# A hybrid decoder step: row projection and recurrence levels in one block, columns projected first

## The reference

```
def even_project(x, pos, lb, w_in):
    h = x @ w_in
    hq, hf, hi, hg, nq, ncmp, nslc, nwin, ngate = jnp.split(h, np.cumsum(EVEN_SPLITS)[:-1], axis=-1)
    f = lb + (1.0 - lb) * jax.nn.sigmoid(hf.astype(jnp.float32))
    hg_q = jax.nn.silu(hq.astype(jnp.float32)).reshape(B, T, HG_HEADS, HG_DK)
    hg_k = 1.0 - f
    hg_lf = jnp.log(f)
    hg_v = hi.astype(jnp.float32).reshape(B, T, HG_HEADS, HG_DV)
    ...
def hgrn2_chunk(S0, q, k, v, lf):
    b = jnp.cumsum(lf, axis=1)
    diff = b[:, :, None] - b[:, None, :]
    decay = jnp.exp(jnp.where(causal[None, :, :, None, None], diff, -jnp.inf))
    a = jnp.einsum('bthk,btshk,bshk->bhts', q, decay, k)
    o = jnp.einsum('bhts,bshv->bthv', a, v) + jnp.einsum('bthk,bhkv->bthv', q * jnp.exp(b), S0)
    S = jnp.exp(b_end)[..., None] * S0 + jnp.einsum('bshk,bshv->bhkv', k * jnp.exp(b_end[:, None] - b), v)
```

## Time and profile before

| | us |
|---|---|
| median of 3 runs | 2469.85 (2465.31 to 2473.75) |
| profiled execution | 2469.82 |
| its span (first to last instruction) | 2468.0 |
| TensorE busy | 1848.0 (75%) |
| VectorE busy | 1529.8 (62%) |
| ScalarE busy | 553.8 (22%) |
| GpSimd busy | 721.3 (29%) |
| DMA, mean | 304 GB/s |

### The profile page before, as it was taken

How to read it: one execution, slowest core, us unless ns; L and a number is a source line. 1 busy time by engine, 2 the same in 40 slices (tenths; PEclk the granted TensorE clock), 3 DMA queues, 4 the chain that set the end, 5 groups by cost and what they waited for, 6 DMA issues and landing times.

```text
span 2468.0 us, 18705 instructions
## 1 busy us (share of the span) xinstructions
PE 1848.0 (75%) x5407; PEld 851.8 (35%) x5407; DVE 1529.8 (62%) x3388; ACT 553.8 (22%) x1694; POOL 721.3 (29%) x612
## 2 busy tenths in 40 slices
PE   8968289899668786686876787685668678688765
PEld 3456155534313222343422342232333233223221
DVE  0053733138498947666578679748757965647976
ACT  0010222101223311222114222313312322212222
POOL 4000000000234533233323334423323434344442
PEclk9985556598789997778988899897889989899988
DMA  8300120300588999999999999999899999999997
GB/s 282 97 18 1 38 69 0 135 35 1 211 334 344 421 420 392 356 370 375 415 403 373 405 415 420 404 413 359 312 369 412 420 373 419 411 421 421 416 382 304
DMA packets 144944, 750.82 MB, mean 304 GB/s; under 512 B 22077, under 2 KB 46537, under 8 KB 63817
## 3 DMA queue, kind: packets, MB, share of 16 engines
q0 software_dynamic: 84480, 608.21, 61.0%
q1 hardware_dynamic: 60360, 141.41, 15.6%
HBM read 743.96 MB, written 5.60 MB: 304 GB/s over the span
## 4 chain that ended last, share of the span: by engine, by line
DMA 22%; DVE 20%; PE 18%; issue 5%; SPq 1%; ACT 1%; POOL 1%; PEldq 1%; DVEq 1%; PEld 0%; ACTq 0%
DMA uv<-in_experts_dram,slots 14%; PE ps L1933 9%; DVE uv L1841 7%; PE ps L525 4%; DVE acc L1855 2%; DMA last_w<-in_odd_w_in_dram 2%; DMA first_w<-in_odd_w_in_dram 2%; PE ps L846 1%; PE ps L685 1%; SPq L1546 1%; PE ps L874 1%; DVE route_s L1675 1%; DMA out_dil_p_dram<-dil_val 1%; DMA last_w<-in_peer_w_q_dram 1%; DMA sample_rows<-in_peer_sub_keys_dram 1%
## 5 line engine op out<-in xcount | busy, mean ns | idle before, releaser
L1823 POOL DMA_INDIRECT uv<-in_experts_dram,slots x576 | 690.7, 1199 | 1685.2 <-PE ps L1933 923.2
L1933 PE MATMUL ps<-uv,diag 128*128 128x512 f32 (+1 forms) x1664 | 897.1, 681 | 286.5 <-ACT diag L1909 222.1
L1841 DVE CUSTOM_DVE_ANT_0 uv<-uv,x 128x1024 f32<-128x1024 f32 x512 | 621.4, 1224 | 360.2 <-DMA uv<-in_experts_dram,slots 278.6
L1933 PEld LDWEIGHTS ps<-uv,diag 128*128 128x128 f32 (+1 forms) x1664 | 314.2, 202 | 783.4 <-issue 446.7
L1887 ACT ACTIVATE gelu<-dot 128x2 f32<-128x2 f32 x288 | 58.6, 203 | 1042.4 <-DVE dot L1841 1041.9
L1855 DVE SCALAR_TENSOR_TENSOR acc<-uv,wgt,acc 128x1024 f32<-128x1024 f32 x155 | 198.4, 1280 | 2.0 <-ACT wgt L1896 2.0
L1896 ACT ACTIVATE wgt<-gate,gelu 128x1 f32<-128x1 f32 x576 | 138.1, 287 | 57.0 <-SPq L2036 23.9
L1909 ACT ACTIVATE diag<-const,wgt 128x128 f32<-128x128 f32 (+1 forms) x416 | 148.7, 386 | 9.4
L1841 DVE CUSTOM_DVE_ANT_0 uv<-uv,xs 128x1024 f32<-128x1024 f32 x64 | 78.1, 1226 | 42.2 <-DMA uv<-in_experts_dram,slots 38.3
L441 PE MATMUL ps<-even_w,xT 128*128 128x512 f32 (+3 forms) x240 | 98.4, 566 | 0.6 <-PEq L288 0.6
L525 PE MATMUL ps<-last_w,xT 128*128 128x512 f32 x160 | 77.3, 626 | 19.1 <-DMA last_w<-in_odd_w_in_dram 16.4
(11 more groups left out here) (430 smaller groups left out, 1931.8 us busy)
## 6 DMA issues: line engine op xcount, KB each, us to landing
sample_cache<-in_cache_dil_kv_dram SPq DMA_DIRECT2D x64, 256.0 KB, 7.5
sample_w_in<-in_odd_w_in_dram SPq DMA_DIRECT2D x12, 1024.0 KB, 11.6
first_w<-in_odd_w_in_dram SPq DMA_DIRECT2D x12, 1024.0 KB, 11.4
last_w<-in_odd_w_in_dram SPq DMA_DIRECT2D x12, 1024.0 KB, 13.4
uv<-in_experts_dram,slots POOLq DMA_INDIRECT x576, 10.7
even_w<-in_even_w_in_dram SPq DMA_DIRECT2D x8, 1024.0 KB, 8.5
uv<-in_peer_w_q_dram SPq DMA_DIRECT2D x8, 1024.0 KB, 13.9
first_w<-in_peer_w_q_dram SPq DMA_DIRECT2D x8, 1024.0 KB, 10.0
```

The source lines that it names most:

```text
L1823: self.k.nc.gpsimd.indirect_dma_start(out=self.uv[:, s % RING, :], out_offset=None, in_=self.table, in_offset=bass.IndirectOffsetOnAxis(ap ...
L1841: ins = nc.vector.tensor_tensor_reduce(self.uv[:, s % RING, 0:D], self.uv[:, s % RING, 0:D], x, 1.0, 0.0, ALU.mult, ALU.add, self.dot[:, g ...
L1933: last = nc.tensor.matmul(k.bank(c)[0:m, :], self.diag[:, s % RING, 0:m], self.uv[:, s % RING, D + 512 * c:D + 512 * (c + 1)], start=(j == ...
```

## The change

The columns are projected before the rows, in a block with the caches' stage and without the rows. The rows move into the recurrence, whose two blocks become one: TensorE does ten pieces of the rows, then one level product after every two pieces, then the rest. Rows use banks 0, 1 and 7 and ScalarE alone for their copies; levels use banks 2 to 5, so the sample tile shares two banks with tile 0 and waits for VectorE's use of them. The rows' buffer `even_w` has three slots and lies at a fixed address, and `q_b` lies in the sigmoid's buffer. The early loads of caches, columns and rows are issued in `load_inputs`, in front of its wait.

```
-def load_inputs(k, x_prompt, x_sample, const):
+def load_inputs(k, x_prompt, x_sample, const, following):
...
             sp.dma_start(k.x[0:NS, 2, :], x_sample.rearrange("b t d -> (b t) d")).then_inc(loaded, 16)
+            for stage in following:
+                stage.parts.pop("early loads")(sp)
             sp.wait_ge(loaded, 48)
...
-def project_rows(k, name, w, widths, out, wbuf, tiles=(0, 1, 2), banks=ALL_BANKS):
+def project_rows(k, name, w, widths, out, wbuf, tiles=(0, 1, 2), banks=ALL_BANKS, by=("vector", "scalar")):
...
-                            pe.wait_ge((v_out, s_out)[(i - nb) % 2], (i - nb) // 2 + 1)
+                            pe.wait_ge(outs[(i - nb) % n_by][0], (i - nb) // n_by + 1)
...
-        q_b = k.sbuf("hg_q_b", [128, C4, DEC_B, NS], ctx=ctx)
+        q_b = sg[:, :, :].rearrange("p a t -> p (a t)")[:, 0:C4 * DEC_B * NS].rearrange("p (c b t) -> p c b t", c=C4, b=DEC_B)
...
+        def level_bank(t, odd):
+            return k.bank(4 + odd if t == 1 else 2 + odd)
+
+        def levels(pe):
+            for n in range(len(LEVELS) + 1):
+                for t in lanes(n):
+                    pe.wait_ge(factors[t] if n else s["prepared"], n or 1)
+                    if t == 2:
+                        pe.wait_ge(factors[0], n + 1)
+                    elif t == 0 and 0 < n <= s_levels:
+                        pe.wait_ge(factors[2], n)
+                    for hd in range(HG):
...
+                    last.then_inc(products[t], 1)
+                    yield
...
         with nc.Block() as block:
+            @block.sync
+            def _(sp):
+                rows.parts["sync"](sp)
+
             @block.tensor
             def _(pe):
                 pe.wait_ge(inputs.landed, 16 * inputs.loads)
-                nc.tensor.transpose(k.bank(0)[:, 0:12], inputs.gamma[:, :], k.c("ident")[0:12, 0:12]).then_inc(s["gamma_turned"], 1)
+                nc.tensor.transpose(k.bank(6)[:, 0:12], inputs.gamma[:, :], k.c("ident")[0:12, 0:12]).then_inc(s["gamma_turned"], 1)
+                dense, small_work = rows.run("tensor", pe), levels(pe)
+                for _ in range(10):
+                    next(dense)
+                for _ in small_work:
+                    for _ in range(2):
+                        next(dense)
+                for _ in dense:
+                    pass
...
                 nc.scalar.activation(small[:, 16:28], small[:, 16:28], ACT.Exp).then_inc(s["bounds_exp"], 1)
+                for _ in rows.run("scalar", act):
+                    pass
...
+                nc.vector.memset(k.pad[:, :], 0.0).then_inc(s["prepared"], 1)
...
+            wbuf = k.nc.alloc_sbuf_tensor_at("even_w", [128, 3, 4, 512], F32, offset=TOP - 4 * 3 * 4 * 512)
+            out = lambda j, t: h[0:ROWS[t], t, 512 * j:512 * j + widths[j]]
+            rows = project_rows(k, "even", w_in[:, 1024:], widths, out, wbuf, (0, 1, 2), (0, 1, 7), ("scalar",))
             with ExitStack() as load:
-                wbuf = k.sbuf("even_w", [128, 4, 4, 512], ctx=load)
                 wbuf_T = k.sbuf("even_wT", [128, 3, 8, 256], ctx=load)
-                out = lambda j, t: h[0:ROWS[t], t, 512 * j:512 * j + widths[j]]
-                rows = project_rows(k, "even", w_in[:, 1024:], widths, out, wbuf)
                 columns = project_cols(k, "even_T", w_in, 1024, hT, wbuf_T)
-                alone(k, transpose_x(k, "x0"), following=(rows,))
-                alone(k, caches.stage(k, state_inputs, a), rows, following=(columns,))
-                alone(k, columns)
-            recurrence(k, h, hT, cat, state_inputs, fin, new, a["hg_norm_g"][0], o["state_prompt"], o["state_sample"])
+                prepare = caches.stage(k, state_inputs, a)
+                load_inputs(k, a["x_prompt"], a["x_sample"], a["const"], (prepare, columns, rows))
+                alone(k, transpose_x(k, "x0"))
+                alone(k, prepare, columns, loads=(columns, prepare))
+            recurrence(k, h, hT, cat, state_inputs, rows, fin, new, a["hg_norm_g"][0], o["state_prompt"], o["state_sample"])
```

More of the change, by code:

```diff
@@ L399, in project_rows @@
     landed = [k.sem(name, f"w_landed{i}") for i in range(slots)]
-    half_done, product, v_out, s_out = [k.sem(name, n) for n in ("half_done", "product", "v_out", "s_out")]
-    n_t = len(tiles)
+    half_done, v_out, s_out = [k.sem(name, n) for n in ("half_done", "v_out", "s_out")]
+    n_t, n_by = len(tiles), len(by)
+    copies = {"vector": (v_out, nc.vector.tensor_copy), "scalar": (s_out, nc.scalar.copy)}
+    outs = [copies[engine] for engine in by]
     loads = [(j, half) for j in range(len(widths)) for half in range(2)]
@@ L450, in take_out @@
             for what, *rest in tick:
-                if what == "leave" and rest[0] % 2 == side:
+                if what == "leave" and rest[0] % n_by == side:
                     i = rest[0]
@@ L457, in take_out @@
             yield
-    stage.on("vector")(lambda dve: take_out(dve, 0, v_out, nc.vector.tensor_copy))
-    stage.on("scalar")(lambda act: take_out(act, 1, s_out, nc.scalar.copy))
+    for side, engine in enumerate(by):
+        stage.on(engine)(lambda eng, side=side: take_out(eng, side, *outs[side]))
     return stage
@@ L1002, in load, with recurrence @@
             sp.dma_start(self.state[:, c, :, :], state[0, :, 2 * c:2 * c + 2].rearrange("b h k v -> (h k) b v")).then_inc(self.landed, 16)
-def recurrence(k, h, hT, cat, inputs, fin, new, norm_g, state_prompt, state_sample):
+def recurrence(k, h, hT, cat, inputs, rows, fin, new, norm_g, state_prompt, state_sample):
     nc, step = k.nc, k.dve_steps
@@ L1014, in recurrence @@
         "gamma_turned", "bounds_diff", "bounds_exp", "sigmoid", "cross_product", "spread", "state_product", "out_product",
-        "state_ready", "squares", "root", "gates")}
+        "state_ready", "squares", "root", "gates", "prepared")}
     products, factors = [[k.sem(f"hg_{n}_tile{t}") for t in range(TILES)] for n in ("products", "factors")]
@@ L1044, in _ @@
                 dve.wait_ge(s["gamma_turned"], 1)
-                step(nc.vector.tensor_copy(small[:, 0:12], k.bank(0)[:, 0:12]))
+                step(nc.vector.tensor_copy(small[:, 0:12], k.bank(6)[:, 0:12]))
                 step(nc.vector.tensor_tensor(small[:, 12:16], small[:, 0:4], small[:, 4:8], ALU.max))
@@ L1105, in _ @@
                         if t < 2:
-                            src = k.ps[:, 2 * t:2 * t + 2, :].rearrange("p a (b t) -> p (a b) t", t=128)
+                            src = k.ps[:, 2 + 2 * t:4 + 2 * t, :].rearrange("p a (b t) -> p (a b) t", t=128)
                             nc.vector.copy_predicated(att[:, t, :, :], bc(masks[:, n, :], 1, HG), src)
@@ L1126, in _ @@
                 dve.wait_ge(s["cross_product"], 1)
-                step(nc.vector.tensor_copy(cross[:, :, :], k.ps[:, 6:8, :].rearrange("p a (b t) -> p (a b) t", t=128)))
+                step(nc.vector.tensor_copy(cross[:, :, :], k.ps[:, 2:4, :].rearrange("p a (b t) -> p (a b) t", t=128)))
                 tN = tot[len(LEVELS) % 2]
@@ L2192, in build @@
         k.level_masks = a["level_masks"]
-        load_inputs(k, a["x_prompt"], a["x_sample"], a["const"])
         w_out = a["even_w_out"][0]
```

40 lines of the change are left out of this document (15 added, 25 removed).

## The result

The changed kernel takes 2436.88 us (median of 4 runs, 2433.36 to 2443.95), the kernel before 2468.51 us beside it: a ratio of 0.9873, 95% interval 0.9845 to 0.9902, 31.6 us less. The forecast was 2452.2 us with a range of 2439 to 2463. The sign was right; the gain is nearly twice the forecast, and the time lies 2 us under the range.

A forecast was written before the change was run, and what follows sets the result against it. TensorE bounds the projections, VectorE and ScalarE the gates, VectorE the levels. Replacing 187.5 us by 5.0 + 41.5 + 124.6 = 171.1, with 1.2 more off, saves 17.6 from 2469.82: 2452.2 us, range 2439 to 2463.

The forecast's parts named there:

- Behind it: Key transposes and first head, right after dense work: 1.2 us taken off, bounds 0 and 15.
- rival C: Recurrence heads keep the full clock after the dense block: 15 us less instead of 1.2, 2438 us; chance 0.04.
- The start: Seven more load issues before SyncE's wait, held by the queue, delay turning x by 5.0 us, bounds 0 and 7.4.
- Rival B: At the start, SyncE isn't held, or the queue holds more: 5.0 us less, 2447.2 us; chance 0.08.
- the sentence of the Trainium skill cited beside the term: Many descriptors can be emitted before their generating cost shows; by that the start's issues are short, sum 5.0 us lower.
- The columns' block: Column projection with GpSimd's page gathers, which end the block: 41.5 us, not 32.0; TensorE idles 9.5 us.
- The merged block: Row projection interleaved with gates and level products: 124.6 us, of it 98.43 rows, 24 products, 0.9 slow clock.
- D: Merged block: small products in the dense stream lower the clock, so slower; 2493 us if a third fell; chance 0.04.
- E: Merged block: no overlap, TensorE waits each round or weight loads come late; 2468 us; chance 0.04.

The follow-up runs named there:

- late: Changed kernel with GpSimd's 32 page gathers moved from the columns' block into the merged block; 2437.98 us, ratio 0.9862 to the kernel before.
- behind: Changed kernel with only the loads of x ahead of SyncE's wait, pages and first column and row weights issued later; 2433.78 us, ratio 0.9839.
- gap: Changed kernel with eight VectorE fills between key transposes and heads, TensorE idle there; 2464.51 us, ratio 0.9966 to the kernel before.
- bridge: Kernel before, plus ten dense products with unused results behind the cross product, ahead of key transposes and heads; 2461.04 us, ratio 0.9971.
- att_fill: Changed kernel plus sixteen dense unused products under VectorE's rotation of queries and keys, ahead of the attention; 2443.90 us, ratio 0.9888.

## Why the prediction was right in sign and wrong in size

**The step that failed** is the term "Behind it", 1.2 us with bounds 0 and 15: it left seven of the eight heads at half clock. The 1.2 is what the key transposes got (3.83 us with their barrier before, 2.54 after, 1.3 less). The heads got another 12.6 us (31.94 before, 19.32 after) and what lies behind them 1.3. The mechanism was on the list as rival C, with 0.04, and against it stood one reading: at 222 to 230 the heads run at 0.50 with TensorE wholly busy. That stretch lies behind the fall. The row shows that heads at 0.50 stay there; it doesn't show that they can't have the full clock, which the first head of the same kernel has (207.70 to 210.10). The question was whether the heads keep the level when they follow dense work, and on that the kernel before has no row, since nothing dense stands ahead of its heads. So C couldn't be refuted from it, and with the bound of 15 us written down it belonged inside the range. Experiments 1 and 2 show the cause from both sides: the old kernel with dense work right ahead has fast heads, the new one with a gap of 11 us has slow ones. But dense work followed by two short idle times, which is what the changed kernel has, doesn't always keep the level: `late` has the same and loses it. With `late`'s heads the term would have been 1.4 us (70.7 from keys to cat, against 72.2 before), as forecast. That the changed kernel keeps the level in each of its profiles is shown; why it does and `late` doesn't is open, and nothing in the change was made for it.

**The start**, forecast +5.0, bounds 0 and 7.4, measured +7.5. The mechanism was right; the size of the queue was not. SyncE's timeline and its queue's packets until 18 us answer to the earlier trace rows:

```profile
3.01 8.89 SPq L566 DMA_DIRECT2D even_wT<-in_even_w_in_dram  x3
11.95 6.25 SPq L419 DMA_DIRECT2D even_w<-in_even_w_in_dram  x3
...
q1 hardware_dynamic: 3218, 5.40, 86.7%
```

The last issue ends at 18.2. By then some 3,280 of the 5,200 packets had moved: 1,920 were outstanding, not the 2,773 counted in the kernel before, and at some 345 packets per us (1,835 by 14 us, 3,218 by 18) the 850 more are 2.5 us. The pace that I had taken (340) was right. Rival B is refuted, and the sentence of the Trainium skill cited beside the term, which writes of GpSimd's path, doesn't carry over to these issues.

**The columns' block**, 41.5 forecast, 44.1 measured. The gathers take 24.42 to 64.21, 39.79 us as in the earlier trace rows, and `late` shows that they end the block. But gamma follows 3.36 us behind the last gather's row, not 0.8:

```profile
63.26 0.95 POOL L1317 DMA_INDIRECT cache_slc<-in_cache_slc_kv_dram,page_rows  x1 [0.30 <-issue]
```

In `behind` it is 55.50 + 0.95 to 60.78, 4.3 us. Since `late` takes out the gathers alone and gamma then follows the columns by 0.74 us, I read this as GpSimd coming to the barrier later than its last row's end; what it does there no row shows.

**The merged block**, 124.6 forecast, 121.4 measured. Its groups (records, busy time, mean):

```profile
L445 PE MATMUL ps<-even_w,xT 128*128 128x512 f32 (+3 forms) x240 | 102.2, 574 | 0.0
L1051 PE MATMUL ps<-hT,hg_key 64*128 64x128 f32 (+1 forms) x304 | 19.9, 271 | 0.0
L1059 PE MATMUL ps<-hT,hg_key 64*128 64x128 f32 x16 | 1.2, 285 | 0.0
```

Rows take 3.8 us over the 98.43 of the earlier trace rows. The slow beginning, costed at 0.9 with bounds to 2.5, is 2.7 of it: in `late`, where the block begins at 1.00, rows take 99.5. From the first product at 88.14 to the block's last at 188.26 it is 100.1 us; 50 of 60 pieces are 82, so 20 products cost some 18 net, near the lower bound of 17 and not 24, since the changes between pieces and products cost nothing that can be seen. That the gates fit under ten pieces and that TensorE never waits were right; D and E are refuted by the 113.00 of 113.00 us busy at 1.00.

**Together**: +1.5 us at the keys (+2.5 at the start, -0.4 at x, +2.6 in the columns' block, -3.2 in the merged block), -14.0 from keys to cat, -2.5 in the rest: 15 us of span, and 15.3 between the forecast and the median. The three larger errors up to the keys are 2.5 to 3.2 us each, of both signs; that only 1.5 us is left of them is luck.

**What stays open**: what decides whether a short idle time costs the level (the moment, or what ran before the merged block), and whether the pools would keep it if none stood ahead of them.

## What to carry to other kernels

Before costing a stage at the clock that it has, ask what TensorE does right ahead of it: here a stretch of small products ran at 0.50 to its end once it was there (25 to 34 us), and with dense work directly in front it held 1.00 for 19 us, so that even useless dense work of 7 to 11 us paid for itself. The level at entry is not enough: three profiles entered at 1.00 and lost it in the second head. A row that shows a stage slow at one level is no evidence on the other, and a bound of 15 us on a term belongs in the range, not in a rival of 4 in 100. When a block is split, list what each of its engines still has to do: GpSimd's 40 us of gathers, hidden under 98 us of projection before, became the end of a 31 us block.

## What was unexpected of the hardware

- The granted clock of a busy TensorE can stay at 0.50 for 34 us (`gap`) or at 1.00 for 19 us (`bridge`) under the same eight heads.
- The same instructions with the same idle times ahead lost the full clock when they began at 176.5 us (twice) and kept it at 184.37, 185.87 and 190.3 to 191.8. Moving work earlier by 15 us so gained nothing (`late`).
- The clock also fell under back-to-back pools, at 278 us in `att_fill`, 3.7 us after they began.
- By the packet counts SyncE was let go with some 1,920 packets outstanding at the start of the changed kernel, and with 2,773 at 85.65 us of the kernel before: the count that holds it isn't one number.
- A barrier that GpSimd ends let TensorE go 3.4 to 4.3 us behind the end of GpSimd's last gather's row.
